# A transformer kernel on one core: group norms applied behind the output projection, head outputs split inside the attention, the next residual added by GpSimd

## What is computed

```python
out_a = global_attention(qa, ka, va)          # 8 heads of 64
out_b = window_attention(qb, kb, vb, sink_b)  # 8 heads of 64
mixed = jnp.concatenate([rms_norm(out_a, group_norm_a),
                         rms_norm(out_b, group_norm_b)], axis=-1) @ w_out
x = x + rms_norm(mixed, norm_mix_post)
h = rms_norm(x, norm_ffn_pre)
f = (jax.nn.silu(h @ w_gate) * (h @ w_up)) @ w_down
x = x + rms_norm(f, norm_ffn_post)

def rms_norm(x, g):   # over the last axis
    return x * lax.rsqrt(jnp.mean(x * x, axis=-1, keepdims=True) + EPS) * g
```

## Time and profile before

| | |
|---|---|
| median of three runs | 2241.54 us |
| the profiled execution | 2241.29 us |
| its span, first to last instruction | 2239.5 us |
| TensorE busy | 2036.5 us, 91% of the span |
| VectorE busy | 1083.6 us, 48% |
| ScalarE busy | 493.5 us, 22% |
| GpSimd busy | 1138.1 us, 51% |
| chain that ended last | TensorE 78%, VectorE 14%, ScalarE 3%, issue 3%, GpSimd 1% |
| attention of the second block | 1597 to 1748 us |
| joint, then projection | 1748 to 1768, 1768 to 1822 us |
| next joint, with the FFN's first unit | 1822 to 1849 us |

### The profile page before, as it was taken

The page is one execution under the profiler, slowest core; times in us unless marked ns, Lnnn a source line. Parts: engine busy times, 40 slices in busy tenths (PEclk is TensorE's granted clock), DMA queues, the critical chain, the costliest instruction groups (busy, mean ns, idle before and its releaser), DMA issues.

```text
span 2239.5 us, 25794 instructions
## 1 busy us (share of the span) xinstructions
PE 2036.5 (91%) x8981; PEld 1644.4 (73%) x8981; DVE 1083.6 (48%) x1375; ACT 493.5 (22%) x897; POOL 1138.1 (51%) x664
## 2 busy tenths in 40 slices
PE   7999999788689899798999999998899679999996
PEld 6888887566477678686778888876677458888884
DVE  6343510565665638866653433029866444433103
ACT  3111001322233422342121110012356321111001
POOL 4666665255133145503666666664545136666661
PEclk9999999889889899999999999999999889999998
DMA  4333233122021123201233333333100022333330
GB/s 145 97 100 94 94 103 87 56 76 73 22 57 47 28 57 86 83 1 47 85 94 95 102 94 94 101 90 85 53 1 1 17 59 85 94 97 100 94 94 37
DMA packets 259800, 163.73 MB, mean 73 GB/s; under 512 B 30380, under 2 KB 249582, under 8 KB 259614
## 3 DMA queue, kind: packets, MB, share of 16 engines
q1 hardware_dynamic: 258080, 157.90, 24.3%
q10 hardware_dynamic: 1662, 5.06, 0.7%
HBM read 160.81 MB, written 2.13 MB: 73 GB/s over the span
## 4 chain that ended last, share of the span: by engine, by line
PE 78%; DVE 14%; ACT 3%; issue 3%; POOL 1%; DMA 0%; ACTq 0%; POOLq 0%; DVEq 0%; SPq 0%
PE bank L639 16%; PE bank L640 16%; PE bank L641 16%; PE bank L706 5%; PE bank L707 5%; PE bank L708 5%; DVE work L1675 3%; PE bank L768 2%; PE bank L660 1%; PE bank L1026 1%; PE bank L1028 1%; PE bank L1027 1%; DVE rowmax L1636 1%; DVE work L1531 1%; PE bank L811 1%
## 5 line engine op out<-in xcount | busy, mean ns | idle before, releaser
L570 POOL TENSOR_SCALAR w_hi<-raw 128x1024 fp32r<-128x1024 f32 x298 | 323.1, 1084 | 971.1 <-PE bank L641 722.5
L572 POOL TENSOR_TENSOR w_lo<-raw,w_hi 128x1024 fp32r<-128x1024 f32 x298 | 745.3, 2501 | 24.9
L639 PE MATMUL bank<-u_hi,w_hi 128*128 128x512 f32 x1632 | 666.3, 408 | 45.0 <-DVE u_lo L1555 18.8
L640 PE MATMUL bank<-u_lo,w_hi 128*128 128x512 f32 x1632 | 642.6, 394 | 0.0
L641 PE MATMUL bank<-u_hi,w_lo 128*128 128x512 f32 x1632 | 642.2, 394 | 0.0
L639 PEld LDWEIGHTS bank<-u_hi,w_hi 128*128 128x128 f32 x1632 | 310.4, 190 | 135.0 <-issue 43.7
L640 PEld LDWEIGHTS bank<-u_lo,w_hi 128*128 128x128 f32 x1632 | 310.8, 190 | 72.1 <-issue 11.3
L641 PEld LDWEIGHTS bank<-u_hi,w_lo 128*128 128x128 f32 x1632 | 310.3, 190 | 66.0
L706 PE MATMUL bank<-hid_hi,w_hi 128*128 (+1 forms) x480 | 186.7, 389 | 0.0
L707 PE MATMUL bank<-hid_lo,w_hi 128*128 (+1 forms) x480 | 186.7, 389 | 0.0
L708 PE MATMUL bank<-hid_hi,w_lo 128*128 (+1 forms) x480 | 186.7, 389 | 0.0
(11 more groups left out here) (421 smaller groups left out, 2675.9 us busy)
## 6 DMA issues: line engine op xcount, KB each, us to landing
raw<-in_w_in SPq DMA_DIRECT2D x52, 512.0 KB, 3.7
raw<-in_ffn_w_gate SPq DMA_DIRECT2D x44, 512.0 KB, 3.8
raw<-in_ffn_w_up SPq DMA_DIRECT2D x44, 512.0 KB, 3.7
raw<-in_ffn_w_down SPq DMA_DIRECT2D x44, 512.0 KB, 3.4
raw<-in_w_gate SPq DMA_DIRECT2D x22, 512.0 KB, 3.8
raw<-in_w_up SPq DMA_DIRECT2D x22, 512.0 KB, 3.8
raw<-in_w_down SPq DMA_DIRECT2D x22, 512.0 KB, 3.5
raw<-in_w_branch SPq DMA_DIRECT2D x12, 512.0 KB, 3.4
```

What stands on the lines that cost most here:

```text
L570: pool.tensor_scalar(w_hi[:, s, :], raw[:, k, :], 1.0, 1.0, ALU.mult, ALU.mult).then_inc(hi_done, 1)
L572: pool.tensor_tensor(w_lo[:, s, :], raw[:, k, :], w_hi[:, s, :].bitcast(F32), ALU.subtract).then_inc(split_ready, 1)
L639: pe.matmul(outs[:, 0:n], wh, rhs_hi[:, c, :], start=(c == 0), stop=False)
L640: pe.matmul(outs[:, 0:n], wh, rhs_lo[:, c, :], start=False, stop=False)
```

## The change

Four things are changed, all in the second block between attention and last FFN.

1. The output projection multiplies the head outputs times gain, without the norm's factor. The halves (`out_a` in chunks 0 to 3, `out_b` in 4 to 7) go to two banks. VectorE's `join` multiplies each by its group's factor (`W[2]`, `W[3]`) and adds them into `mo`. Three pairs of banks are used in turn; from the fourth unit on, unit m waits for the join of unit m-3. The sums of the group norms are two fp32 matmuls inside unit 1.
2. The head outputs are split inside the attention, some steps after their pair is done: `group_high` on ScalarE (high part, square), `group_low` on VectorE (low part, running sum of squares). `group_high` waits for `a_out`, `group_low` for `group_high`. The eighth chunk follows the attention.
3. The sum of squares of the projection's result is kept by VectorE (`add_square(N_POST, ...)`) and summed by TensorE in one fp32 matmul at the end instead of eight.
4. GpSimd adds the scaled chunks to `hT`, after it has split the FFN's first two units; VectorE's adds of squares for the FFN's norm follow all its low parts, out of eight tiles.

```diff
+        ou_hi = at("ou_hi", [P, KC, S], u_at + 16384, F32R)
+        ou_lo = at("ou_lo", [P, KC, S], a_at, F32R)
...
+            if ni == N_FPRE:
+                return mo[:, c, :]
+            if ni == N_GRP:
+                return (W[0], W[1], raw_a[:, 0, :], raw_a[:, 1, :], raw_a[:, 2, :], raw_b[:, 0, :], raw_b[:, 1, :],
+                        turn_tmp[:])[c]
...
+        b2_steps = steps_of(b2_heads)
+        b2_ends = [last_step(b2_steps, 2 * g + 1) for g in range(KC)]
...
-            for u in range(U_WO2 + SPL, U_GU3):
+            for u in range(U_WO2 + SPL, U_GU3 + SPL):
                 one(u)
-            run(U_GU3, N_UNITS)
+            for c in range(KC):
+                pool.wait_ge(n_t, SCALED[N_POST] * KC + c + 1)
+                pool.tensor_tensor(hT[:, c, :], hT[:, c, :], W[4 + c % 2], ALU.add).then_inc(x_ready, 1)
+            run(U_GU3 + SPL, N_UNITS)
...
-            norm_sum(N_GRP, groups=2)
-            pe.wait_ge(n_std, N_GRP + 2)
-            w_out(U_WO2, U, 8, norm_wait(N_GRP), lambda m: amid(4, lambda: sum_chunk(N_POST, m - 1, SUM_BANK)))
-            sum_chunk(N_POST, KC - 1, SUM_BANK)
+            def group_sum(ab):
+                pe.wait_ge(n_acc, N_GRP * KC + KC - 2)
+                pe.matmul(bank[6 + ab][:], ones, W[ab], start=True, stop=True).then_inc(n_acc, 1)
+
+            def w_out_2():
+                for m in range(KC):
+                    slot, b = m % SPL, 2 * (m % 3)
+                    if m >= 3:
+                        pe.wait_ge(res, KC + m - 2)
+                    pe.wait_ge(split_ready, U_WO2 + m + 1)
+                    for c in (0, 4, 1, 5, 2, 6, 3, 7):
+                        if m == 0:
+                            pe.wait_ge(n_lo, SPLITS[N_GRP] * KC + 2 * (c % 4) + c // 4 + 1)
+                        if m == 1 and c == 1:
+                            group_sum(0)
+                            group_sum(1)
+                        o = bank[b + c // 4][:]
+                        wh = w_hi[:, slot, c * P:(c + 1) * P]
+                        wl = w_lo[:, slot, c * P:(c + 1) * P]
+                        pe.matmul(o, wh, ou_hi[:, c, :], start=c % 4 == 0, stop=False)
+                        pe.matmul(o, wh, ou_lo[:, c, :], start=False, stop=False)
+                        last = pe.matmul(o, wl, ou_hi[:, c, :], start=False, stop=c % 4 == 3)
+                    last.then_inc(unit_done, 1)
+                sum_total(N_POST, 6)
...
+                def group_high(g):
+                    c = o2_chunk(g)
+                    act.wait_ge(a_out, A_B2[4] + g + 1)
+                    act.activation(ou_hi[:, c, :], o2T[:, c, :], ACT.Identity,
+                                   scale=gain[:, G_GN + c:G_GN + c + 1]).then_inc(n_hi, 1)
+                    act.activation(square_of(N_GRP, g), o2T[:, c, :], ACT.Square).then_inc(n_sq, 1)
+                hooks = {b2_ends[g] + PV_LAG + 4: lambda g=g: group_high(g) for g in range(KC - 1)}
...
+                group_high(KC - 1)
+                load_root()
+                norm_std(N_GRP, groups=2, b=6)
...
-            squares(N_GRP, o2T, lambda c: act.wait_ge(a_out, A_B2[4] + 8))
-            norm_std(N_GRP, groups=2)
-            norm_hi(N_GRP, u_hi)
...
+                def group_low(g):
+                    c = o2_chunk(g)
+                    dve.wait_ge(n_hi, SPLITS[N_GRP] * KC + g + 1)
+                    dve.wait_ge(n_sq, N_GRP * KC + g + 1)
+                    dve.scalar_tensor_tensor(out=ou_lo[:, c, :], in0=o2T[:, c, :], scalar=gain[:, G_GN + c:G_GN + c + 1],
+                                             in1=ou_hi[:, c, :].bitcast(F32), op0=ALU.mult, op1=ALU.subtract).then_inc(n_lo, 1)
+                    if g >= 2:
+                        if g >= 4:
+                            dve.wait_ge(n_acc, N_GRP * KC + g - 3)
+                        dve.tensor_tensor(W[g % 2], W[g % 2], square_of(N_GRP, g), ALU.add).then_inc(n_acc, 1)
...
+                hooks = {b2_ends[g] + PV_LAG + 6: lambda g=g: group_low(g) for g in range(KC - 1)}
...
-            norm_split(N_GRP, N_GRP, o2T, G_GN, u_hi, u_lo, groups=2)
+            def join(m):
+                b = 2 * (m % 3)
+                dve.wait_ge(unit_done, U_WO2 + m + 1)
+                dve.tensor_tensor(mo[:, m, :], bank[b][:], W[2], ALU.mult).then_inc(g_part, 1)
+                if m >= 2:
+                    dve.wait_ge(res, KC + m - 1)
+                dve.tensor_tensor(W[4 + m % 2], bank[b + 1][:], W[3], ALU.mult).then_inc(g_part, 1)
+                dve.wait_ge(g_part, 2 * m + 2)
+                dve.tensor_tensor(mo[:, m, :], mo[:, m, :], W[4 + m % 2], ALU.add).then_inc(res, 1)
+            norm_recip(N_GRP, groups=2)
+            dve.wait_ge(n_rec, N_GRP + 2)
             for m in range(KC):
-                dve.wait_ge(unit_done, U_WO2 + m + 1)
-                dve.tensor_copy(mo[:, m, :], bank[m % 4][:]).then_inc(res, 1)
-            norm_add(N_POST, N_POST + 1, mo, G_POST2, KC, lambda c: (gained_low(N_FPRE, G_FPRE2, c), add_square(N_FPRE, c)))
-
+                join(m)
+                if m:
+                    add_square(N_POST, m - 1)
+            add_square(N_POST, KC - 1)
+
+            norm_recip(N_POST + 1)
+            dve.wait_ge(n_rec, N_POST + 2)
+            for c in range(KC):
+                if c >= 2:
+                    dve.wait_ge(x_ready, KC + c - 1)
+                dve.scalar_tensor_tensor(out=W[4 + c % 2], in0=mo[:, c, :], scalar=gain[:, G_POST2 + c:G_POST2 + c + 1],
+                                         in1=W[2], op0=ALU.mult, op1=ALU.mult).then_inc(n_t, 1)
+                if c >= 2:
+                    gained_low(N_FPRE, G_FPRE2, c - 2)
+            gained_low(N_FPRE, G_FPRE2, KC - 2)
+            gained_low(N_FPRE, G_FPRE2, KC - 1)
+            for c in range(KC):
+                add_square(N_FPRE, c)
```

More of the change, by code:

```diff
@@ L250, in two_blocks @@
         c_stored = sem("c_stored")
-        tab_scaled, qa_raw = sem("tab_scaled"), sem("qa_raw")
+        tab_scaled, qa_raw, g_part = sem("tab_scaled"), sem("qa_raw"), sem("g_part")
         hi_done = sem("hi_done")
@@ L665, in sum_total @@
                 pe.wait_ge(n_acc, ni * KC + KC - 1)
-                pe.matmul(bank[b][:], ones, W[3], start=True, stop=True).then_inc(n_acc, 1)
+                pe.matmul(bank[b][:], ones, total_of(ni), start=True, stop=True).then_inc(n_acc, 1)
             def norm_sum(ni, n=S, groups=1):
@@ L1162, in norm_hi, with square_in @@
                     act.activation(dst[:, c, :], W[4 + c % 2][:, 0:n], ACT.Copy).then_inc(n_hi, 1)
+            def square_in(ni, c, src):
+                if c >= 2 and ni not in (N_PRE, N_FPRE):
+                    act.wait_ge(n_acc, ni * KC + max(1, c - 2))
+                act.activation(square_of(ni, c), src[:, c, :], ACT.Square).then_inc(n_sq, 1)
             def gained_hi(ni, g0, ready, b=SUM_BANK, eager=True):
                 def square(c):
-                    if c >= 2 and ni != N_PRE:
-                        act.wait_ge(n_acc, ni * KC + max(1, c - 2))
-                    act.activation(square_of(ni, c), hT[:, c, :], ACT.Square).then_inc(n_sq, 1)
+                    square_in(ni, c, hT)
                 for c in range(KC):
@@ L1564, in add_square @@
                     dve.wait_ge(n_acc, ni * KC + c - 1)
-                dve.tensor_tensor(W[3], square_of(ni, 0) if c == 1 else W[3], square_of(ni, c), ALU.add).then_inc(n_acc, 1)
+                total = total_of(ni)
+                dve.tensor_tensor(total, square_of(ni, 0) if c == 1 else total, square_of(ni, c), ALU.add).then_inc(n_acc, 1)
             def ffn(fi, u0, ni, std_no, finish, between=None):
@@ L1747, in norm_add @@
                         add(c - 1)
-                    if c >= 2 and also:
-                        also(c - 2)
                 add(KC - 1)
-                if also:
-                    also(KC - 2)
-                    also(KC - 1)
             dve.memset(gain_rows[:], 0.0).then_inc(gain_zero, 1)
@@ L2064, in put @@
                 def put(r, g):
-                    return o2T[r, (g % 2) * 4 + g // 2, :]
-                attend(A_B2, b2_heads, put, part="first")
-                attend(A_B2, b2_heads, put, part="rest", lows=False, hooks={
-                    0: lambda: value_low(S_B2 + V_A, ast, 6), 1: lambda: raw_v_of(1), 2: lambda: turn_a(4),
-                    3: lambda: (low_b(4), low_a(4)), 5: lambda: value_low(S_B2 + V_B, bst, 5)})
-            mixer_in()
-            norm_split(N_GRP, N_GRP, o2T, G_GN, u_hi, u_lo, groups=2)
@@ new lines, in mixer_in @@
+                attend(A_B2, b2_heads, put, part="first")
+                hooks = {b2_ends[g] + PV_LAG + 6: lambda g=g: group_low(g) for g in range(KC - 1)}
+                hooks |= {0: lambda: value_low(S_B2 + V_A, ast, 6), 1: lambda: raw_v_of(1), 2: lambda: turn_a(4),
+                          3: lambda: (low_b(4), low_a(4)), 5: lambda: value_low(S_B2 + V_B, bst, 5)}
+                attend(A_B2, b2_heads, put, part="rest", lows=False, hooks=hooks)
```

(2 more changed lines are left out.)

20 lines of the change are left out of this document (14 added, 6 removed).

## The result

| | before | changed |
|---|---|---|
| median of four runs each | 2242.94 us | 2229.25 us |
| the profiled execution (its span) | 2241.29 (2239.5) | 2231.07 (2229.1) |
| TensorE, VectorE busy | 91%, 48% | 91%, 51% |
| GpSimd, ScalarE busy | 51%, 22% | 52%, 22% |

The changed kernel takes 0.994 of the time, 95% interval 0.9923 to 0.9958: 13.7 us less by the medians, against 19.4 forecast. It lies in the range, nearer to its upper end.

The account below looks back on a forecast made before the run. At the second block's joints TensorE's matmuls wait some 25 us behind a norm. From 2241.29 us, 31.2 − 3.6 − 2.85 − 4.2 − 1.2 = 19.4 us gain gives 2221.9 us; range 2213 to 2232, forecast's own 2215 to 2229.

Parts of the forecast that it names:

- part 1: Output projection before the norm: last head's copy to last unit's take-up falls from 79.2 to 48.0 us, gain 31.2 us.
- the six covered hooks: Splits inside the attention, groups 0 to 5: 1.0 us at each window pair, 0.2 at the others, loss 3.6 us.
- the seventh: Hook in the last heads of the attention, without cover from row maxima: last copy comes 2.85 us later.
- the join's tail: After the projection's last unit: the join's add waits for GpSimd, 10.8 us to first scaled chunk instead of 6.6, loss 4.2.
- the residual: Residual stretch: GpSimd's adds take turns with VectorE, 2.4 us a chunk, 20.4 us instead of 19.2, loss 1.2 us.
- signs of being wrong: Attention growing by over 10 us, chunk pace of 1.5 us, or TensorE waiting for the squares' sum in third FFN unit.
- part 3: The join on VectorE: covered inside the loop, exposed after the last unit, where its SBUF add can't run beside GpSimd; loss 4.2 us.
- (a): Rival: GpSimd's residual adds run free of VectorE, the stretch falls from 20.4 to 14 us; 2216 us, chance 0.08.
- (b): Rival: ScalarE's blocked hooks cost 2.6 us at each of six covered places, 15.6 us; 2234 us, chance 0.10.
- (c): Rival: each of seven hooks delays TensorE by ScalarE's whole hold, 4.5 us; 2247 us, slower, chance 0.04.
- (d): Rival: ScalarE reloads tables twice at each of seven hooks, 1.28 us each, 18 us; 2240 us, chance 0.02.
- (e): Rival: joins and weight splits block each other, projection units stay above 5.44 us, 6 us lost; 2228 us, chance 0.06.

Follow-up runs that it names:

- E1: Changed kernel with VectorE's half of the hook (`group_low`) one step later, behind the next head's shift matrix; 2223.51 us.
- E2: Changed kernel with both hook halves later: ScalarE's `group_high` two steps, VectorE's `group_low` one step; 2220.04 us.
- E7: E6 with the seventh pair's split also moved behind the attention, so only six pairs are split inside it; 2212.95 us.
- E5: Changed kernel with GpSimd's weight split of the FFN's second unit held until VectorE has added the last square of the projection's result; 2228.00 us.
- E4: Changed kernel with the residual add back on VectorE, adds of squares still after the last split; 2228.05 us.
- E9: E8 with the residual add on GpSimd again, as in the changed kernel; 2215.11 us.
- E11: E8 with VectorE's adds of squares for the FFN's norm between the chunks again, as in the kernel before; 2213.97 us.
- E8: The kernel of E7 once more, unaltered, as the measure for three kernels that each take one mend out; 2211.59 us.
- E6: Changed kernel with three mends together: both hook halves later, residual add on VectorE, weight split gated; 2215.00 us.
- E10: E8 with GpSimd's weight split of the FFN's second unit not gated, as in the changed kernel; 2214.63 us.

## Why the prediction was right, and where it missed

The terms against what they measured in the region: part 1 1.6 us short, the six covered hooks 4.5, the seventh 0.1, the join's tail 1.0 short, the residual 1.1 better; together 6.1 of the 19.4 us, which leaves 13.3. One of the prediction's own signs of being wrong came true: the attention grew by 11.0 us, over the 10 it had named and outside the 0 to 7 it had allowed there. The time still lies in the stated range because that range was wide: 2229.25 us is a hair above the forecast's own 2215 to 2229, and what lies above that had been taken in on other grounds. As far as the attention goes, that the range held is luck.

**The direction and part 1: right.** The bet was that 31 us of exposed norm go and some 12 come back. The first matmul follows the last copy at once, units are 5.44 us apart, unit 3 never waits for a bank. The term was 48.0 us, measured 49.6; E1, with 48.0, shows what the 1.6 is: the second fall of the clock, priced at 2 us and left to the range.

**Part 2, the six covered hooks: the term that was mis-sized.** 3.6 us forecast, 8.1 measured (the first six intervals). The sum had two statements. The hold of ScalarE, 1.0 us at each window pair, was about right: in E1, where VectorE's half is out of the way and TensorE doesn't wait for the shift, these three intervals are 0.77, 0.75 and 0.76 longer than before. The failed step is the sentence that VectorE's `group_low` stands ahead of `diagonal` and "hides there". I had set its duration against TensorE's slack and forgotten GpSimd, though part 3 used that very port. The hold makes GpSimd's three low parts fall into the stretch where VectorE makes the shift, and each instruction there waits its turn: 2.1 us at the fourth and the sixth pair, 0.5 at the second. Together with the hold that is 2.9 for each of the two pairs with an add.

The even hooks were taken at 0.2. The first is (17.62 against 17.43). At the third and fifth the clock must be looked at: in before, the interval from the third to the fourth multiply has a granted clock of 0.90 and takes 17.46 us, and the like one from the fifth to the sixth has 1.00 and takes 16.28. In the changed kernel both have 1.00 and take 17.29. At the fifth the hook thus costs 1.0 us. At the third no row of before has the clock at 1.00; by an estimate from the 16.28 us of the fifth, the hook costs 1.0 there too, and a clock that stood higher than before pays for it, which no term had foreseen. Why it stood higher isn't shown. (In E1 the third interval takes 17.88 us at 1.00 and the fifth 17.55 at 0.90.) First before, then the changed kernel, busy time by stretch:

```profile
1668.00:1685.40 17.40, 15.90 (x72) 13.48 (x72) 12.10 (x19) 10.63 (x22) 8.96 (x8) 0.90 0.00 0
1702.90:1719.10 16.20, 14.58 (x72) 11.92 (x72) 12.10 (x19) 10.63 (x22) 8.92 (x8) 1.00 0.01 2
```

```profile
1672.30:1689.60 17.30, 15.02 (x72) 11.92 (x72) 15.43 (x21) 11.14 (x23) 9.08 (x8) 1.00 0.00 0
1710.00:1727.20 17.20, 15.03 (x72) 11.93 (x72) 15.38 (x21) 11.14 (x23) 9.09 (x8) 1.00 0.00 1
```

**The seventh hook: right.** 2.85 us forecast, 2.9 measured. E2 and E7 split it: 1.45 goes when the hook is put later, so that ScalarE isn't held, and 1.45 when its extra work goes as well.

**The join's tail: right mechanism, 1 us short.** 4.2 forecast, 5.2 measured. The collision of the join's add with GpSimd came as worked out (2.84 us; gone in E5). The sum of squares was priced at 1.0 us; behind 5.66 us idle it ran at the lower clock (0.50) and took 2.08.

**The residual: right.** VectorE and GpSimd alternate as the port pair of the earlier trace rows said; 20.4 us forecast, 19.4 measured, since the handoffs are shorter than I took them. That the residual stretch stayed as long as before hides two things that cancel: GpSimd's add costs 3.5 us (E4, E9) and moving the squares' adds out of the loop saves 3.4 (19.24 in before, 15.85 in E4), 1.7 by the region where TensorE begins to wait for their sum (E11). The cover of 8.5 us for them held without a stall in the changed kernel (the sum starts 8.4 us behind the last split) and was overrun by 1.21 us in E8. A sentence of the Trainium skill that I had not weighed goes further than my "reads two SBUF tensors": "SBUF — State Buffer", section "Who interferes with whom", says that a VectorE `tensor_scalar` can use both ports as well and then contends with GpSimd. The shift matrix is one, with a single tensor read, and its rows agree: 0.87 us alone, 2.86 and 3.93 beside GpSimd.

**The rivals.** (a), free adds, is out by the alternating rows. (b), hooks of 2.6 us each, was wrong in mechanism but near in size at two of six. (c) and (d) did not occur: no hook cost 4.5 us, and no table load stands at a hook. (e) is out, at 5.44 us a unit.

**A version that beats both:** the kernel of E7 and E8, 2211.59 us in its second set of runs, 1.4% below before and some 17 us below the changed kernel: six hooks where they hold nobody, the residual add on VectorE, the weight split gated.

## What to carry to other kernels

Before an instruction is put ahead of others in an engine's order, list what waits behind it there and what *their* consumers then do all at once: a hold of one engine bunches the work of the next, and the bunch collides. Put such work one or two steps later, where its operand is ready, before doubting the work itself (11.0 us became 2.4). Moving an elementwise operation from VectorE to GpSimd gains nothing where both must use the shared port in one chain; gate off-path work of GpSimd out of an exposed tail instead.

## What the hardware showed beyond that

The granted clock is sensitive to small things. In the changed kernel and in E1, TensorE has the same 8 us of full clock behind the last copy and the same gap of 1.9 us before the eighth chunk; in the one the clock then falls to 0.54 for 3.7 us, in the other it stays at 1.00. The sum of squares shows the same: behind 3.50 us idle it takes 1.12 us in E8 and 2.08 in E6. I can't say from these rows what decides it. One such fall made 1.6 us, the other 0.95, as much as many an edit.

The part of the kernel that no edit touches begins its last third anywhere within 3.5 us, 1497.06 to 1500.61 in the traces. A difference of 1 us between two medians of five runs (E4, E5) is then no evidence, while the same edits show in the region of the traces at 3.4 and 2.5 us, and in medians within one set, E9 and E10 against E8, at 3.5 and 3.0 (0.95 of the latter is the clock). Where this scatter arises stays open.
